# A hybrid decoder step on one core: learned tokens leave the stages whose output drops them

## What is computed

```
q, k, v, iq, ik, iw, za, cu, zc, gt = split(x @ w_in)
ik = layer_norm(ik);  ga, gb = split(cu);  u = ga * sigmoid(gb)
scores = sum over 16 heads of iw * relu(iq . ik)       # indexer
sel    = top 128 (prompt) or top 130 (samples) keys by scores, causal
attn   = softmax over sel of (q . k - slope * distance) @ v
c      = depthwise causal convolution of u, 31 taps
a_br   = (attn * silu(za)) @ w_att_out
c_br   = (silu(layer_norm(c)) * silu(zc)) @ w_conv_out
mixed  = sigmoid(gt0) * a_br + sigmoid(gt1) * c_br
y      = layer_norm(2**0.25 * x + mixed @ w_o)
y_prompt = y without the learned tokens
```

## Time and profile before

| | |
|---|---|
| median of 3 executions | 1761.26 us (1760.91 to 1761.4) |
| the profiled execution | 1760.29 us |
| its span, first to last instruction | 1758.4 us |
| mean granted TensorE clock | 0.993 |
| busy: TensorE, VectorE, ScalarE, POOL | 1711.9, 698.0, 430.5, 606.6 us |

### The profile page before, as it was taken

One profiled execution on the slowest core, in us unless ns is written; L12 is line 12 of the kernel. 1 busy time (PEld: TensorE's weight loads), 2 busy tenths in 40 slices (PEclk: granted clock), 3 DMA queues, 4 the chain that ended last, 5 costly groups with the idle time before them and its releaser, 6 DMA issues.

```text
span 1758.4 us, 29192 instructions
## 1 busy us (share of the span) xinstructions
PE 1711.9 (97%) x11521; PEld 1596.5 (91%) x11521; DVE 698.0 (40%) x1608; ACT 430.5 (24%) x532; POOL 606.6 (34%) x178
## 2 busy tenths in 40 slices
PE   7999999999999999999999999999989999999996
PEld 5899749999999989889999999999989999977774
DVE  2012577822221011012889999807552222110017
ACT  3112441123323212121121221221451211231110
POOL 3233103333222232234445454465333343333331
PEclk9999989999999999999999999999999999999998
DMA  6333023332332443452322333333326434532212
GB/s 210 94 95 100 5 69 93 81 94 73 90 86 70 141 128 100 118 143 74 96 72 72 88 82 81 89 79 88 93 69 192 137 100 150 179 124 83 84 48 108
DMA packets 245933, 174.74 MB, mean 99 GB/s; under 512 B 17979, under 2 KB 224283, under 8 KB 244363
## 3 DMA queue, kind: packets, MB, share of 16 engines
q1 hardware_dynamic: 241211, 163.64, 32.8%
q10 hardware_dynamic: 4608, 9.70, 1.5%
HBM read 157.15 MB, written 16.89 MB: 99 GB/s over the span
## 4 chain that ended last, share of the span: by engine, by line
PE 92%; DVE 3%; ACT 1%; issue 1%; DMA 1%; SPq 1%; POOL 0%; ACTq 0%; DVEq 0%; POOLq 0%
PE ps L1490 70%; PE ps L1477 14%; PE ps L1697 1%; PE ps L1706 1%; PE ps L1653 1%; PE ps L1557 1%; DVE y L1445 1%; DVE y L1451 1%; DMA raw<-in_w_conv_out_dram 1%; PE ps L1671 0%; DVE bias L1158 0%; DVE xlo L1396 0%; PE ps L1526 0%; ACT xhi L1047 0%; DMA xn<-in_x_prompt_dram 0%
## 5 line engine op out<-in xcount | busy, mean ns | idle before, releaser
L676 POOL TENSOR_TENSOR wlo<-raw,whi 128x2048 fp32r<-128x2048 f32 (+1 forms) x116 | 532.8, 4593 | 1001.1 <-ACT whi L749 1001.1
L1490 PE MATMUL ps<-xhi,whi 128*128 128x296 f32 x3040 | 665.9, 300 | 1.7 <-ACT bias L852 1.0
L1490 PE MATMUL ps<-xhi,wlo 128*128 128x296 f32 x3040 | 662.4, 299 | 0.0
L1490 PE MATMUL ps<-xlo,whi 128*128 128x296 f32 x3040 | 660.7, 299 | 0.0
L1490 PEld LDWEIGHTS ps<-xhi,whi 128*128 128x128 f32 x3040 | 493.5, 189 | 4.0 <-issue 2.0
L1490 PEld LDWEIGHTS ps<-xlo,whi 128*128 128x128 f32 x3040 | 494.1, 189 | 0.0
L1490 PEld LDWEIGHTS ps<-xhi,wlo 128*128 128x128 f32 x3040 | 492.4, 188 | 0.0
L749 ACT ACTIVATE whi<-raw 128x2048 fp32r<-128x2048 f32 (+1 forms) x116 | 221.3, 1908 | 181.8 <-PE ps L1477 170.1
L1477 PE MATMUL ps<-whi,mhi 128*128 128x512 f32 (+1 forms) x320 | 126.7, 396 | 0.5 <-POOL wlo L738 0.5
L1477 PE MATMUL ps<-wlo,mhi 128*128 128x512 f32 (+1 forms) x320 | 125.5, 392 | 0.0
L1477 PE MATMUL ps<-whi,mlo 128*128 128x512 f32 (+1 forms) x320 | 125.4, 392 | 0.0
(11 more groups left out here) (262 smaller groups left out, 1223.6 us busy)
## 6 DMA issues: line engine op xcount, KB each, us to landing
raw<-in_w_in_dram SPq DMA_DIRECT2D x84, 1024.0 KB, 5.7
raw<-in_w_o_dram SPq DMA_DIRECT2D x16, 1024.0 KB, 5.1
gate<-gates_dram SPq DMA_DIRECT2D x16, 592.0 KB, 6.5
raw<-in_w_att_out_dram SPq DMA_DIRECT2D x16, 512.0 KB, 4.2
raw<-in_w_conv_out_dram SPq DMA_DIRECT2D x16, 512.0 KB, 5.5
gates_dram<-tmp_gate ACTq DMA_DIRECT2D x24, 296.0 KB, 2.2
vpage<-in_cache_v_dram SPq DMA_DIRECT2D x32, 128.0 KB, 2.0
kpage<-in_cache_k_dram SPq DMA_DIRECT2D x32, 128.0 KB, 2.1
```

The costliest lines, as they stand in the source:

```text
L676: nc.gpsimd.tensor_tensor(wlo[:, buf, 0:width], raw[:, buf, 0:width], whi[:, buf, 0:width].bitcast(F32), ALU.subtract).then_inc(lo_ready, 1)
L1490: ins = mm(ps[:, bank + half, 0:HALF], w[b][:, k, :], x[:, k, half * HALF:(half + 1) * HALF], start=(k == k0 and m == 0), stop=(k == k0 + ...
```

## The change

`OUTT` names the 576 columns without the learned tokens, `OUTW` their number, `OUTH` half of it, 288.

1. Queries, gates, both SiLU paths and the branch blocks take the columns of `OUTT` alone, in halves of 288. All that is evicted, stored, combined and normalized behind them shrinks with it (592 to 576). The `ga` and `gb` blocks keep all 592, since the convolution reads the learned tokens; the convolution's own sums start behind them (2 x 264 columns become 2 x 256). Columns of `qT` that are no longer written are cleared by POOL, ahead of the low split of the third query block, and TensorE waits for that once the queries are through.
2. The indexer queries also leave out the first 128 tokens: 464 columns are left, in one bank and one product.
3. In the output projection the row tiles shift by the 16 tokens: four of 128 prompt rows, and a fifth of the 64 sample rows. For the fifth, the high and low halves stand side by side in `mboth` and act as one stationary of 128 columns: one product makes high by high in rows 0 to 63 and low by high in rows 64 to 127, a second adds high by low. VectorE evicts the two row halves in turn, and writes the low part of the branches as two instructions.
4. On SyncE the store of `ikiw` and the 24 small loads move ahead of the load of the first query block.
5. The `N_CU` stretch loops over 12 blocks instead of 4, as two kinds of blocks now follow each other.

Cut to the core:

```diff
+OUTT = slice(META, TOK)
+OUTW = TOK - META
+OUTH = OUTW // 2
+YROWS = [P, P, P, P, OUTW - 4 * P]
+IQ0 = P
+IQW = TOK - IQ0
...
+    mixed = at("mixed", [P, KC, 2 * OUTW], F32R, B0)
+    mhi = mixed[:, :, 0:OUTW]
+    mboth = mixed[:, :, SEQ:SEQ + 2 * DB * DS]
+    mlo = mixed[:, :, SEQ + 2 * DB * DS:]
...
             load_tiles(N_IQ, 8, CUT["iq"])
+            sp.wait_ge(ikiw_ready, 2)
+            sp.dma_start(iw_dram[:, :], ikiw[0:ROWS[4], 4, IDIM:]).then_inc(iw_stored, 16)
+            sp.wait_ge(iw_stored, 16)
+            for h in range(IH):
...
             load_tile(N_Q, CUT["q"], N_Q % 2)
...
-            with pool.Fori(0, (N_ZA - N_IQ) // 2) as i:
+            with pool.Fori(0, (N_Q + 2 - N_IQ) // 2) as i:
                 for b in range(2):
                     split_lo(N_IQ + b + i * 2, (N_IQ + b) % 2)
+            pool.wait_ge(idx_stored, 16 * 6)
+            pool.wait_ge(hi_ready, N_Q + 3)
+            nc.gpsimd.memset(qT[:, :, 0:META], 0.0).then_inc(q_cleared, 1)
+            with pool.Fori(0, (N_ZA - N_Q - 2) // 2) as i:
...
-                nc.scalar.activation(xhi[:, k, :], qT[:, k, :] if k < 8 else zc[:, k - 8, :], ACT.Copy
+                nc.scalar.activation(xhi[:, k, OUTT], qT[:, k, OUTT] if k < 8 else zc[:, k - 8, OUTT], ACT.Copy
...
-                nc.vector.tensor_tensor(mlo[:, j, :], m_tmp[:, j % 2, :], mhi[:, j, :].bitcast(F32), ALU.subtract
-                                        ).then_inc(mlo_ready, 1)
+                nc.vector.tensor_tensor(mlo[:, j, :], m_tmp[:, j % 2, 0:SEQ], mhi[:, j, 0:SEQ].bitcast(F32),
+                                        ALU.subtract).then_inc(mlo_ready, 1)
+                nc.vector.tensor_tensor(mboth[:, j, DB * DS:], m_tmp[:, j % 2, SEQ:], mhi[:, j, SEQ:].bitcast(F32),
+                                        ALU.subtract).then_inc(mlo_ready, 1)
...
+                    if t == 4:
+                        link(nc.vector.scalar_tensor_tensor(dst, ps[r:2 * r, (Y_BANK + t) % 8, :], 0.5, dst,
+                                                            ALU.mult, ALU.add))
                     nc.vector.scalar_tensor_tensor(dst, ps[0:r, (Y_BANK + t) % 8, :], 0.5, dst, ALU.mult, ALU.add
...
+                        if r == DB * DS:
+                            ends = last and k == 3
+                            both = (ps[:, (bank + t) % 8, :], mboth[:, k0 + k, :], w[0][:, k, :])
+                            high = (ps[0:r, (bank + t) % 8, :], mboth[:, k0 + k, 0:r], w[1][:, k, :])
+                            mm(*(high if ends else both), start=(first and k == 0), stop=False)
+                            ins = mm(*(both if ends else high), start=False, stop=ends)
+                            continue
...
-            def tile_block(buf, bank, k0=0, kn=KC):
+            def tile_block(buf, bank, k0=0, kn=KC, t0=META, width=OUTH):
...
-                        for half in range(2):
-                            ins = mm(ps[:, bank + half, 0:HALF], w[b][:, k, :],
-                                     x[:, k, half * HALF:(half + 1) * HALF],
+                        for half in range((TOK - t0) // width):
+                            ins = mm(ps[:, bank + half, 0:width], w[b][:, k, :],
+                                     x[:, k, t0 + half * width:t0 + (half + 1) * width],
...
+                if isinstance(n0, int) and N_CU <= n < N_G2 and kind_at(n)[0] in ("ga", "gb"):
+                    cols = dict(t0=0, width=HALF)
+                tile_block(n % 2, 2 * b, **cols).then_inc(block_used, 1)
...
-            tile_pair(N_IQ, 0)
+            tile_pair(N_IQ, 0, t0=IQ0, width=IQW)
...
             tiles(N_Q, 8)
+            pe.wait_ge(q_cleared, 1)
```

More of the change, by code:

```diff
@@ L143, in build @@
           k_sample, v_sample, idx_k_sample, conv_sample):
-    gates = nc.dram_tensor("gates_dram", [32, P, TOK], F32)
+    gates = nc.dram_tensor("gates_dram", [32, P, OUTW], F32)
     iw_dram = nc.dram_tensor("iw_dram", [ROWS[4], IH], F32)
@@ L496, in _ @@
             load_tiles(N_IQ, 8, CUT["iq"])
+            sp.wait_ge(ikiw_ready, 2)
+            sp.dma_start(iw_dram[:, :], ikiw[0:ROWS[4], 4, IDIM:]).then_inc(iw_stored, 16)
+            sp.wait_ge(iw_stored, 16)
+            for h in range(IH):
+                p0 = 64 * (h % 2) + DS * (h // 2)
+                sp.dma_start(wcol[p0:p0 + DS, :], iw_dram[LAST:ROWS[4], h:h + 1].rearrange("(b t) o -> t (b o)", t=DS),
+                             allow_slow_non_contiguous=True).then_inc(wcol_here, 16)
+            for j in range(IH // 2):
+                sp.dma_start(wcol_last[LAST * j:LAST * (j + 1), :], iw_dram[0:LAST, 2 * j:2 * j + 2]
+                             ).then_inc(wcol_here, 16)
             load_tile(N_Q, CUT["q"], N_Q % 2)
@@ L633, in _ @@
             sp.wait_ge(block_used, N_WO)
[L634 to L639, removed]
+            for t in range(4):
+                sp.dma_start(y[:, t, :], x_prompt[0, t * P:(t + 1) * P, :]).then_inc(y_here, 16)
+            sp.dma_start(y[0:YROWS[4], 4, :], x_sample.rearrange("b t d -> (b t) d")).then_inc(y_here, 16)
             for v, dst in ((ln_post_g, post_g), (ln_post_b, post_b)):
@@ L801, in take @@
                 def take(i, b):
[L802 removed]
+                    j = i * 2 + b + first
+                    dst = iqT[:, j, IQ0:TOK] if isinstance(j, int) else \
+                        iqT[:, ds(j, 1), IQ0:TOK].rearrange("p a t -> p (a t)")
+                    nc.scalar.activation(dst, ps[:, 2 * b, 0:IQW], ACT.Copy).then_inc(tile_taken, 1)
                 return take
@@ L1327, in _ @@
                         bd = dwT[:, ds(j, 1), CW:CW + 1].rearrange("p a k -> p (a k)")
-                        nc.vector.tensor_scalar(out_p[0], row[:, 0:H0], w, bd, ALU.mult, ALU.add
+                        nc.vector.tensor_scalar(out_p[0], in_p[0], w, bd, ALU.mult, ALU.add
                                                 ).then_inc(conv_step, 1)
-                        nc.vector.tensor_scalar(out_p[1], row[:, H0:LP], w, bd, ALU.mult, ALU.add
+                        nc.vector.tensor_scalar(out_p[1], in_p[1], w, bd, ALU.mult, ALU.add
                                                 ).then_inc(conv_step, 1)
@@ L1462, in rows_block @@
             def rows_block(n, buf, act_hi, act_lo, k0, first, last, out_sem, empty=None, ready=True,
-                           some=range(TILES), bank=0, quarters=False):
+                           some=range(TILES), bank=0, heights=YROWS, quarters=False):
                 if ready:
@@ L1571, in _ @@
             ins.then_inc(ikiw_out, 1)
-            tiles(N_IQ + 2, 6)
+            tiles(N_IQ + 2, 6, t0=IQ0, width=IQW)
             pe.wait_ge(tile_taken, 8 + 2)
@@ L1812, in _ @@
                     ins.then_inc(state_out, 1)
-            tiles(N_CU, N_TAIL - N_CU)
+            turn = 4 * CU_STEP
+            turns = (N_TAIL - N_CU) // turn
+            with pe.Fori(0, turns) as i:
+                for b in range(turn):
+                    one_tile(N_CU + b - b % 2, b % 2, i * (turn // 2))
+            for n in range(N_CU + turn * turns, N_TAIL):
+                one_tile(n - (n - N_CU) % 2, (n - N_CU) % 2)
             pe.wait_ge(state_taken, 4)
```

162 lines of the change are left out of this document (75 added, 87 removed).

## The result

| | before | after |
|---|---|---|
| median | 1761.32 us (4 executions) | 1697.24 us (4 executions, 1696.2 to 1698.42) |
| ratio | | 0.9636, 95% interval 0.9625 to 0.9648 |
| profiled execution, its span | 1760.29, 1758.4 us | 1698.42, 1696.6 us |
| mean granted TensorE clock | 0.993 | 0.990 |

The forecast was 1700.5 us with a range of 1696 to 1709. From profiled execution to profiled execution 61.9 us came off, where the sum had 60.8. Nearly all of the rest of the distance to 1697.24 is the profiled execution's own place among the runs: before it was 0.97 us under the median, after it is 1.18 above. That the totals agree says little yet; by stage some terms were well off.

What follows compares the result with a forecast made beforehand. TensorE's long product stretches were taken as the bound. 24.3 + 23.5 + 0.3 + 12.9 − 0.3 + 0.1 = 60.8 us off the profiled 1760.29 gave 1699.5, plus 0.97 to the median: 1700.5 us, range 1696 to 1709.

Steps and rivals of the forecast that it cites:

- What bounds the kernel: Long unbroken TensorE stretches of tile and row projections, TensorE busy 97%; the end moves by what is taken out of them.
- Price of a column: TensorE products priced by moving columns, 0.436 ns each between 296 and 512 columns; 3.49 ns for 8 columns.
- Indexer queries: Eight indexer tiles go from 96 products of 296 columns to 48 of 464, saving 24.3 us.
- Learned tokens: Halves of 288 instead of 296 columns in 72 tile blocks; 70 in unbroken stretches save 23.5 us.
- Entry, late gates, POOL's clearing: Passage into the branches saves 0.3 us; late gates keep 0.9 us to spare; clearing 16 columns on POOL costs nothing.
- Output projection: Fifth row tile needs two products instead of three; 56 products of 512 columns removed, saving 12.9 us.
- Tail: Last evictions: a second eviction costs 0.7 us, one store fewer gives back 0.43 us; net 0.3 us longer.
- SyncE: Moving one store and 24 small loads ahead of the first query tile's load and the stores costs nothing.
- A: Weight loads, not columns, bound the tile blocks; 23.5 us of narrowing lost, 1724 us; chance 0.04.
- B: Indexer tiles still fed at the old pace by weight splits or late loads; 21.3 us lost, 1722 us; chance 0.05.
- C: One indexer product of 464 columns costs as much as two of 296; 24.3 us lost, 1725 us; chance 0.02.
- D: Slower: low clock level lasts into the query tiles, 12.8 us more each, some 1790 us with seven; chance 0.02.

Runs made afterwards that it cites:

- wide halves: Kernel after the change, with the 72 tile blocks reading two halves of 296 columns again, evictions still 288: 1724.84 us.
- the longer slice: Kernel after the change, with 16 unused columns behind each slice of the mixed-branch and gate buffers, 4672 bytes instead of 4608: 1701.63 us.
- the loop over 6 blocks: Kernel after the change, with the stretch behind the attention looping over 6 blocks instead of 12: 1693.8 us, and 1693.63 us when run again.
- three products: Kernel after the change, with the output projection's fifth row tile in three products of 64 stationary columns again, evicted once: 1708.75 us.
- the small loads behind the stores: Kernel after the change, with SyncE's indexer-weight store and 24 small loads back behind the key and value stores: 1698.22 us.

## Why the prediction was right, and where not

**What bounds the kernel.** Right. The end moved by what left the long stretches.

**Price of a column.** Good for the long step (464 columns forecast 210.0 ns, measured 210.8 to 212.6), too low for the short one: 3.7 to 4.4 ns for 8 columns between like pieces, 4.0 over all by the wide halves, where 3.49 was taken. That is at or above my upper bound too: 3.69 ns, the proportional price. The step that failed is the straight line between 296 and 512; it was read off at 512 from products whose pace, as the longer slice shows, hangs on the layout of the other operand as well. The layout doesn't explain the miss: with its faster pace, 226.7 ns at 512, the line would be flatter, (226.7 − 136.7)/216 x 8 = 3.33 ns. The Trainium skill, TensorE: Matmul & The Clock Gate, section Back-to-back issue gap, gives the slope 1/2.4 ns, 3.33 for 8 columns; the measured step of 4.0 lies further from it than from my 3.49.

**Indexer queries.** Right: 24.1 us on the tiles (81.11 us for 105.21), 24.3 forecast, and no wait for a split in them.

**Learned tokens.** 23.5 forecast; in the table the five stages with the entry gave 22.95 us for 23.8. That is near only because two errors cancel, which is luck: the narrower products brought 27.6 us (wide halves again), and the loop gave 4.1 back. The range was held by the same luck: without the pause the kernel takes 1693.6 to 1693.8 us (the loop over 6 blocks), below its lower end of 1696. The two priced terms of that end reach only 1697.9, and the third, less of the indexer at the low clock level, did not come: the granted clock over the scores is 0.92 in both traces (198 to 262 us before, 174.6 to 238.6 after). The change list had the longer loop as its fifth point, and the prediction gave it no price. It should have: the body no longer repeats without being fetched again, as the packets show. By the rows of before alone it couldn't be sized, since a body of 4 blocks showed no wait; the page of the Trainium skill that is named with the experiments would have given the rival.

**Entry, late gates, POOL's clearing.** No wait for a low-half split in the late gates or the queries; the passage to the output projection saved 5.47 for 5.0. The 0.7 us for the split of the third branch block don't show in this trace, where the last 15 branch blocks run in one piece.

**Output projection.** The shared passes are right (12.7 for 12.9). The layout's 3.0 to 3.4 us were not seen: the prediction took 512 columns at 230.9 ns for given.

**Tail.** Forecast 0.3 us longer, measured 0.44. The last tile in the chain, kernel after:

```profile
1685.66 0.70 DVE y L1455
1686.39 0.69 DVE y L1457
```

The second eviction is 0.7 us as priced; the rest of the tail gave back 0.3 us, where 0.4 were priced for the saved store.

**SyncE.** Right that the reorder costs nothing.

**Rivals.** A is out: 112.0 ns at 232 columns. B is out: indexer tiles at 10.1 us without a wait. C is out by the 464-column pace. D did not come in the query tiles, 12.8 us each; a fall of the clock did come, in another place and for three microseconds.

## What to carry to other kernels

When an edit lengthens a loop, count the instructions of its body on each engine: the pause came at the jump back and vanished with half the body, at no other cost. Price a narrower product from a row at a neighbouring width if there is one, since 8 columns were worth between 2 and 5 ns here. And when a total agrees with the sum, still set the stages side by side: here a gain of 4 us and a loss of 4 us had hidden each other.

## What I had not expected of the hardware

- A jump back over 2304 TensorE instructions paused it for 1.9 to 2.3 us in each of the nine traces with that loop. The granted clock fell to 0.50 behind it for some 3 us in seven of them, and stayed at 1.00 in two (three products, and the small loads behind the stores) after pauses of 2.0 to 2.1 us, within the range of the others. Windows of the latter:

```profile
920.00:921.00 1.00, 0.85 (x6) 0.85 (x7) 1.00 (x4) 1.00 (x1) 0.92 (x2) 1.00 0.09 16
921.00:922.00 1.00, 1.00 (x9) 1.00 (x8) 1.00 (x4) 0.17 (x1) 1.00 (x1) 1.00 0.00 0
```

  The 1536 products behind the pause took 207.2 us there, and 208.5 to 208.7 with the slow start (the run with wide halves aside): 1.5 us of scatter between executions of the same code.
- TensorE started again 1.66 to 1.76 us after the instruction packet had landed in all nine.
- The pace of a product of 512 columns depended on how the stationary operand lay in memory: 226.7 ns with slices of 4608 bytes, 231 to 232 with 2368, 4672 and 4736.
